# Out projection in halves, a group norm on token scalars, and two one-sided tiles

## The reference, cut to what matters

```python
xbc = silu(centred_dwconv(h @ w_in[:, o0:o1], ...))   # x 1024, B 256, C 256 channels
...
for o, gate in enumerate(gates):                      # hyena branch, twice
    z = gate * (fft_conv(z, kf[:, o]) + z * hy_bias[o])
y_hy = rmsnorm(z.reshape(b, L, 8, 128), hy_norm_w)    # 8 groups of 128 channels
y_ssd, s_f, s_b = ssd_branch(...)                     # state-space branch
out = concatenate([y_hy, y_ssd], -1) @ w_out          # 2048 x 2048
x = x + g1 * out
```

## Time and profile before

| what | value |
|---|---|
| median of 3 runs | 4664.4 us (4656.6 to 4666.23) |
| span of the profiled execution | 4666.4 us |
| its own time | not listed apart; the listed runs reach 4666.23 us |
| mean granted PE clock | 0.966 |
| busy share | PE 94%, PEld 79%, POOL 71%, DVE 57%, ACT 37% |
| inverse transforms end, out1 begins | 809.8 us, 846.1 us |
| last out1 matmul starts | 938.8 us |

### The profile page before, as it was taken

How to read it: one execution, slowest core, us unless ns; L and a number is a source line. 1 busy time by engine, 2 the same in 40 slices (tenths; PEclk the granted TensorE clock), 3 DMA queues, 4 the chain that set the end, 5 groups by cost and what they waited for, 6 DMA issues and landing times.

```text
span 4666.4 us, 65475 instructions
## 1 busy us (share of the span) xinstructions
PE 4367.9 (94%) x24574; PEld 3666.7 (79%) x24574; DVE 2647.6 (57%) x3815; ACT 1718.0 (37%) x1864; POOL 3296.1 (71%) x1312
## 2 busy tenths in 40 slices
PE   8898989789999999999989998999999899899997
PEld 1676755668888878888877886899888788788876
DVE  3326675365554575544254412598867857875784
ACT  1234432333333343434434332443333333333333
POOL 0347750668888877877867783887887787787776
PEclk9998979899999999999999998999999999999999
DMA  8346750445555544444544452444554454454443
GB/s 314 128 175 245 298 210 1 154 153 186 183 180 180 186 154 165 173 167 181 190 145 163 171 186 87 170 167 166 178 185 169 158 190 170 162 181 173 171 165 124
DMA packets 111126, 805.19 MB, mean 173 GB/s; under 512 B 12903, under 2 KB 13192, under 8 KB 14088
## 3 DMA queue, kind: packets, MB, share of 16 engines
q1 hardware_dynamic: 108720, 787.30, 46.8%
q10 hardware_dynamic: 2200, 14.90, 0.9%
HBM read 800.06 MB, written 2.10 MB: 172 GB/s over the span
## 4 chain that ended last, share of the span: by engine, by line
PE 34%; POOL 28%; issue 20%; DVE 7%; POOLq 0%; ACT 0%; DMA 0%; DVEq 0%; ACTq 0%
POOL w_lo L430 28%; PE psum L498 18%; PE psum L500 9%; DVE out_hl L2747 2%; PE psum L620 2%; DVE out_hl L2745 1%; DVE hid L2743 1%; PE psum L1145 1%; PE psum L487 1%; PE psum L488 1%; PE psum L489 1%; DVE mix_m L2002 0%; POOLq L427 0%; DVE chosen L2683 0%; DVE pick L2679 0%
## 5 line engine op out<-in xcount | busy, mean ns | idle before, releaser
L430 POOL TENSOR_TENSOR w_lo<-ring,w_hi 128x1024 fp32r<-128x1024 f32 x1216 | 2945.6, 2426 | 1219.5 <-ACT w_hi L1221 1218.5
L1221 ACT ACTIVATE w_hi<-ring 128x1024 fp32r<-128x1024 f32 x1240 | 1310.9, 1060 | 2175.4 <-PE psum L500 1920.9
L498 PE MATMUL psum<-hc_hl,w_hi 128*128 128x512 f32 x5184 | 1865.9, 404 | 82.8 <-DVE hc_hl L2177 24.5
L500 PE MATMUL psum<-hc_hl,w_lo 128*128 128x256 f32 x5184 | 1460.8, 282 | 0.0
L498 PEld LDWEIGHTS psum<-hc_hl,w_hi 128*128 128x128 f32 x5184 | 983.3, 190 | 325.2 <-issue 56.7
L500 PEld LDWEIGHTS psum<-hc_hl,w_lo 128*128 128x128 f32 x5184 | 989.0, 191 | 4.7 <-issue 4.5
L498 PE MATMUL psum<-out_hl,w_hi 128*128 128x512 f32 x2048 | 726.0, 399 | 30.7 <-DVE x L2757 27.3
L500 PE MATMUL psum<-out_hl,w_lo 128*128 128x256 f32 x2048 | 578.9, 283 | 0.0
L498 PEld LDWEIGHTS psum<-out_hl,w_hi 128*128 128x128 f32 x2048 | 388.5, 190 | 123.3 <-DVE x L2757 28.3
L500 PEld LDWEIGHTS psum<-out_hl,w_lo 128*128 128x128 f32 x2048 | 392.1, 191 | 0.0
L498 PE MATMUL psum<-hid_hl,w_hi 128*128 128x512 f32 x1024 | 363.9, 400 | 17.4 <-DVE hid_hl L2231 12.2
(11 more groups left out here) (439 smaller groups left out, 5509.9 us busy)
## 6 DMA issues: line engine op xcount, KB each, us to landing
ring<-stream SPq DMA_DIRECT2D x652, 1024.0 KB, 4.8
ring<-mixed SPq DMA_DIRECT2D x96, 1024.0 KB, 6.5
x<-x ACTq DMA_DIRECT2D x2, 2048.0 KB, 11.2
ctx_raw<-ctx ACTq DMA_DIRECT2D x1, 2048.0 KB, 9.6
mem_raw<-mem ACTq DMA_DIRECT2D x1, 2048.0 KB, 9.2
out<-x SPq DMA_DIRECT2D x4, 512.0 KB, 2.6
filt_w<-filt_w ACTq DMA_DIRECT2D x1, 1024.0 KB, 10.8
dft<-dft ACTq DMA_DIRECT2D x1, 1024.0 KB, 12.7
```

What stands on the lines that cost most here:

```text
L430: pool.tensor_tensor(w_lo[:, slot], ring[:, s, k], w_hi[:, slot].bitcast(F32), ALU.subtract).then_inc(lo_ready, 1)
L498: pe.matmul(psum[:, b, :].rearrange("p (s t) -> p s t", s=2), w_hi[:, slot, c], x_hl, start=start(c), stop=False, skip_group_check=True)
L500: m = pe.matmul(psum[:, b, 0:T], w_lo[:, slot, c], x_hl[:, 0], start=False, stop=stop(c), skip_group_check=True)
L1221: act.activation(w_hi[:, 2 * (s % 2) + h], ring[:, s, k], ACT.Copy).then_inc(hi_ready, 1)
```

## The change

- Out projection: tiles 0 to 3 are done in eight halves, first the state-space halves (blocks 8 to 15) of all four tiles, then their hyena halves. Each tile's PSUM bank stays open between. From tile 4 on the old loop runs. SP reloads a slot after its second half. DVE's first four additions wait for the later halves.
- Group norm of the hyena half: in two channel halves q, each with its own semaphores. PE multiplies the squares (as weights) with a column of ones, 8 products of one column, so that the sums lie by token on partitions, 8 numbers each. Mean, root and reciprocal work on [128, 8]. PE spreads the reciprocals to all partitions: 8 products of 128 columns with the identity. The scaled result is written in PSUM; ACT makes `h_hi` from it, DVE `h_lo`.
- xbc: tiles 10 and 11 (C) are computed for x alone: three 256-column matmuls per block, convolution and silu on 256 columns.
- Semaphores renamed and shared (group norm of both branches, value turning of the memory attention); no work differs there.

```diff
@@ sync
         for s in range(RING):
             slot_free(MIXED - RING + s)
             load(FIRST["out1"] + s, s)
-        with sp.Fori(FIRST["out1"] // RING + 1, N_TILES // RING) as i:
+        for s in range(RING):
+            sp.wait_ge(lo_ready, 2 * XBC + RING + s + 1)
+            load(FIRST["out1"] + RING + s, s)
+        with sp.Fori(FIRST["out1"] // RING + 2, N_TILES // RING) as i:
@@ gpsimd
+        for n in range(2 * RING):
+            t, h = n % RING, 1 - n // RING
+            pool.wait_ge(hi_ready, 2 * XBC + n + 1)
+            if n == 0:
+                pool.wait_ge(y_y, 4)
+            pool.tensor_tensor(w_lo[:, n % 4], ring[:, t, 8 * h:8 * h + 8], w_hi[:, n % 4].bitcast(F32),
+                               ALU.subtract).then_inc(lo_ready, 1)
@@ tensor, xbc
+                    if t >= XBC - 2:
+                        o = psum[:, t % RING, 0:T]
+                        pe.matmul(o, w_hi[:, slot, c], h_hi[:, k], start=k == 0, stop=False)
+                        pe.matmul(o, w_hi[:, slot, c], h_lo[:, k], start=False, stop=False)
+                        m = pe.matmul(o, w_lo[:, slot, c], h_hi[:, k], start=False, stop=k == KC - 1)
+                        continue
@@ tensor, after inverse(3)
+        def group_columns(q):
+            pe.wait_ge(gn_sq, q + 2)
+            for k in range(4):
+                for b in range(2):
+                    m = pe.matmul(psum[:, 4 + 2 * q, 2 * k + b:2 * k + b + 1], hy_sq[:, 4 * q + k, b * P:b * P + P],
+                                  const[:, ONES, 0:1], start=True, stop=True)
+            m.then_inc(gn_sum, 1)
+        def group_spread(q):
+            pe.wait_ge(gn_inv, q + 1)
...
+                    m = pe.matmul(psum[:, 4 + 2 * q + k // 2, c0:c0 + P], hy_n[:, q, n:n + 1].broadcast_to([P, P]),
+                                  sq(IDENT), start=True, stop=True)
+            m.then_inc(gn_spread, 1)
+        def out1_half(n):
+            t, h = n % RING, 1 - n // RING
+            pe.wait_ge(lo_ready, 2 * XBC + n + 1)
+            for c in range(8):
+                if n == RING and c % 4 == 0:
+                    pe.wait_ge(gn_out, c // 4 + 2)
...
-        group_norm_pe(0)
-        pe.wait_ge(gn_out, 1)
-        linear("out1", h_hl)
+        group_columns(0)
+        pe.wait_ge(gn_out, 1)
+        pe.wait_ge(y_zc, 8)
+        out1_half(0)
+        group_columns(1)
+        group_spread(0)
+        out1_half(1)
+        group_spread(1)
+        for n in range(2, 2 * RING):
+            out1_half(n)
+        linear("out1", h_hl, RING, KC - RING)
@@ scalar, after z_out_(3, 1)
+        def out1_split(n):
+            t, h = n % RING, 1 - n // RING
+            act.wait_ge(landed[t], FIRST["out1"] // RING * 16 + 16)
+            act.wait_ge(half_done, 2 * FIRST["out1"] + n - 3)
+            act.activation(w_hi[:, n % 4], ring[:, t, 8 * h:8 * h + 8], ACT.Copy).then_inc(hi_ready, 1)
...
-        group_norm_act(0, u[:, 0:8])
+        act.wait_ge(y_y, 2)
+        for n in range(RING):
+            out1_split(n)
+        half_square(0)        # waits y_new 3, squares u[:, 0:4]
+        half_square(1)        # waits y_new 4
         act.dma_start(x[:], a["x"]).then_inc(norm_in, 16)
-        split_stage("out1", ahead=2)
+        half_root(0)
+        half_root(1)
+        out1_split(4)
+        half_high(0)
+        out1_split(5)
+        half_high(1)
+        out1_split(6)
+        out1_split(7)
+        split_stage("out1", RING, KC - RING)
@@ vector, after next_z(3)
-        group_norm_dve(0)
...
+        half_mean(0)
+        half_inverse(0)
+        half_mean(1)
+        half_inverse(1)
+        half_scaled(0)        # 4 x [128, 256]: PSUM <- u, hy_norm, PSUM
+        half_scaled(1)
+        half_low(0)           # [128, 1024]: h_lo <- PSUM, h_hi
+        half_low(1)
@@ vector, residual (all out-projection additions)
-            with dve.Fori(0, n // RING - 1) as i:
+            for j in range(RING):
+                add(0, j, RING - 1 - j)
+            with dve.Fori(1, n // RING - 1) as i:
```

More of the change, by code:

```diff
@@ L327, in build @@
         "inverse", "new_z"))
-    gn_in, gn_sq, gn_sum, gn_ms, gn_rt, gn_out = (sem("gn_" + n) for n in ("in", "sq", "sum", "ms", "rt", "out"))
+    gn_sq, gn_sum, gn_ms, gn_rt, gn_out = (sem("group_norm_" + n) for n in ("sq", "sum", "ms", "rt", "out"))
+    gn_scaled, gn_hi, gn_inv, gn_spread = (sem("group_norm_" + n) for n in ("scaled", "hi", "inverse", "spread"))
     hid_ready = sem("hidden_ready")
@@ L840, in _ @@
         inverse(3)
[L842 to L847, removed]
-            m.then_inc(gn_sum, 1)
-        group_norm_pe(0)
-        pe.wait_ge(gn_out, 1)
-        linear("out1", h_hl)
+        def group_columns(q):
[4 more added lines that the diff above has]
+                                  const[:, ONES, 0:1], start=True, stop=True)
+            m.then_inc(gn_sum, 1)
+        def group_spread(q):
+            pe.wait_ge(gn_inv, q + 1)
+            for k in range(4):
+                for b in range(2):
+                    n = 2 * k + b
+                    c0 = (k % 2) * T + b * P
+                    m = pe.matmul(psum[:, 4 + 2 * q + k // 2, c0:c0 + P], hy_n[:, q, n:n + 1].broadcast_to([P, P]),
[7 more added lines that the diff above has]
+                    pe.wait_ge(gn_out, c // 4 + 2)
+                pe.matmul(psum[:, t, :].rearrange("p (s t) -> p s t", s=2), w_hi[:, n % 4, c], h_hl[:, :, 8 * h + c],
+                          start=h == 1 and c == 0, stop=False, skip_group_check=True)
+                m = pe.matmul(psum[:, t, 0:T], w_lo[:, n % 4, c], h_hi[:, 8 * h + c], start=False,
+                              stop=h == 0 and c == 7, skip_group_check=True)
+            m.then_inc(half_done, 1)
+        group_columns(0)
+        pe.wait_ge(gn_out, 1)
+        pe.wait_ge(y_zc, 8)
[7 more added lines that the diff above has]
+        linear("out1", h_hl, RING, KC - RING)
         norm_pe("x2")
@@ L942, in _ @@
             if n == 29:
-                group_norm_pe(1)
+                pe.wait_ge(gn_sq, 4)
+                for k in range(8):
+                    m = pe.matmul(psum[:, 4 + k // 2, (k % 2) * T:(k % 2) * T + T], sq(ONES), gn_q[:, k],
+                                  start=True, stop=True)
+                m.then_inc(gn_sum, 1)
         def dil_rotate(h, p):
@@ L1309, in xbc_silu @@
             act.wait_ge(bank_free, 4 + bank_of["xbc"] + t + 1)
-            act.activation(xbc[:, t], xbc[:, t], ACT.Silu).then_inc(s_silu, 1)
+            v = xbc[:, t, 0] if t >= XBC - 2 else xbc[:, t]
+            act.activation(v, v, ACT.Silu).then_inc(s_silu, 1)
         for t in range(2, XBC):
@@ L1539, in _ @@
             if n == 5:
-                act.wait_ge(gn_out, 2)
+                act.wait_ge(gn_out, 4)
                 act.dma_start(dil_mask[:], a["dil_mask"]).then_inc(s_tab, 16)
@@ L1912, in _ @@
         for t in range(XBC):
-            conv_base[0] = st.n - 4 * t
-            conv_tile(t // RING, t % RING, FIRST["xbc"], xbc[:, t].rearrange("p s t -> p (s t)"), "ssd_w", "ssd_b", XBC, True)
-            st.n += 4
+            pair = t < XBC - 2
+            conv_base[0] = st.n - (4 if pair else 2) * t
+            conv_tile(t // RING, t % RING, FIRST["xbc"],
+                      xbc[:, t].rearrange("p s t -> p (s t)") if pair else xbc[:, t, 0], "ssd_w", "ssd_b", XBC, pair)
+            st.n += 4 if pair else 2
             if t == 3:
@@ L2141, in _ @@
         st.settle()
-        dve.tensor_tensor(h_lo[:, 8:16], y_ssd[:], h_hi[:, 8:16].bitcast(F32), ALU.subtract).then_inc(g_out, 1)
-        dve.wait_ge(g_out, 1)
+        dve.tensor_tensor(h_lo[:, 8:16], y_ssd[:], h_hi[:, 8:16].bitcast(F32), ALU.subtract).then_inc(gn_out, 1)
+        dve.wait_ge(gn_out, 1)
         filter_parts(1)
@@ L2159, in _, with half_mean, half_inverse, half_scaled @@
         next_z(3)
[L2161 to L2170, removed]
-        group_norm_dve(0)
[L2172 to L2177, removed]
+        def half_mean(q):
+            dve.wait_ge(gn_sum, q + 2)
+            dve.tensor_scalar(hy_n[:, q], psum[:, 4 + 2 * q, 0:8], 1.0 / P, EPS, ALU.mult, ALU.add).then_inc(gn_ms, 1)
+        def half_inverse(q):
+            dve.wait_ge(gn_rt, q + 2)
+            dve.reciprocal(hy_n[:, q], hy_n[:, q]).then_inc(gn_inv, 1)
+        def half_scaled(q):
+            ps = flat[:, 2048 + 1024 * q:3072 + 1024 * q]
+            dve.wait_ge(gn_spread, q + 1)
+            for k in range(4):
+                m = dve.scalar_tensor_tensor(ps[:, T * k:T * k + T], u[:, 4 * q + k], col("hy_norm", 4 * q + k),
+                                             ps[:, T * k:T * k + T], ALU.mult, ALU.mult)
+            m.then_inc(gn_scaled, 1)
+        def half_low(q):
+            dve.wait_ge(gn_hi, q + 1)
+            dve.tensor_tensor(h_lo[:, 4 * q:4 * q + 4].rearrange("p k t -> p (k t)"),
+                              flat[:, 2048 + 1024 * q:3072 + 1024 * q],
+                              h_hi[:, 4 * q:4 * q + 4].bitcast(F32).rearrange("p k t -> p (k t)"),
```

(5 more changed lines are left out.)

63 lines of the change are left out of this document (33 added, 30 removed).

## The result

| what | before | with the change |
|---|---|---|
| median | 4664.4 us (4656.6 to 4670.82, 5 runs) | 4624.8 us (4618.79 to 4643.73, 5 runs) |
| ratio | | 0.9912 [0.9895, 0.9929] |
| profiled execution | span 4666.4 | span 4625.2, its own time 4627.06 |
| inverse transforms end | 809.9 us | 799.5 us |
| last out1 matmul starts | 938.84 us | 897.83 us |

Faster by 39.6 us by the medians and 41.2 by the two spans; forecast was 43.3. Of the 41.2, 41.0 are there when out1 ends (938.84 - 897.83). The interval of the ratio is 33 to 49 us, so the total alone can't tell 43.3 from 39.6.

The account below looks back on a forecast made before the run. PE, 94% busy, was taken as the bound, so gains come from less PE work or filled pauses. xbc 12.9 (10.2 + 1.3 + 1.4) plus tail 30.4 made 43.3 us: span 4623.1, median 4621, range 4610 to 4636.

Parts of the forecast that it names:

- The total and the sign: Whole program: faster by 43.3 us, median 4621; forecast itself had chance 0.73, faster by more than 9 us 0.95.
- xbc's matmuls, 10.2 us: xbc tiles 10 and 11: three narrow matmuls replace 0.68 us a block, 2 x 16 x 0.32 = 10.2 us saved.
- The 1.4 us of clock: Behind xbc's last convolution: pause falls from 2.97 to 1.7 us, so 1.4 us of half clock returns (bounds 0 and 1.4).
- They should follow: Mixed stage after xbc: it should follow the earlier start, passing on the sum of 12.9 us (bounds 11.5 and 12.9).
- the xbc gain is lost in the mixed stage: First rival, mixed stage: its loads or POOL sums set the end whatever PE does; 4634 us, chance 0.08.
- The lock: Tail: `u` (two SBUF inputs on DVE) waits for the POOL instruction under way; second u 1.6 us late, PE stalls 1.5.
- so I expect full clock: xbc's shortened pause: after a pause of 2.22 us PE ran its next 256-column matmul in 0.28 us, the full-clock value.
- the lock or the clock costs more: Second rival, tail: POOL's four halves hold DVE, or clock falls at the stall; up to 9.4 us more, 4630, chance 0.14.
- The tail, 30.4 us: Inverse transforms to out1's end: 908.6 against 938.96, 30.4 us saved, 2.5 of it late clock; bounds 21 and 31.9.
- Table load: ACT before the root: load of 1.28 us with nothing behind it; with the page's drain the sum is 41.9, not 43.3.
- What was costed at nothing: Tail: h copies covered with 1.2 us to spare before hyena half 4; reloads of 4.8 us covered by the eight halves.
- The slower rival: Out1: PE's clock does not hold, a half takes 2.3 us more, 73 us over 32 halves; 4694, chance 0.02.

Follow-up runs that it names:

- h1: The changed kernel with out1's second half put on PE ahead of the second group-norm column sums, POOL's lock left in place; 4625.29 us, one run.
- t1: The changed kernel without the narrow C tiles, so only the new tail (halves and group norm) against the kernel before; 4633.63 us, ratio 0.9927.
- p1: The changed kernel with two more POOL waits, so no POOL instruction lies over DVE's product writing the second `u`; 4626.2 us, ratio 0.9899.
- x1: The kernel before with only xbc's tiles 10 and 11 computed for x alone, tail as before; 4655.01 us, ratio 0.9977.
- x2: x1 with the old 512-column convolution of tiles 10 and 11, silu still 256 columns wide; 4657.1 us, one run.
- r1: The changed kernel run again without an edit; 4631.8 us, ratio 0.9919.
- r2: The changed kernel run again without an edit, beside z1 on the same chip, five rounds; 4624.03 us, ratio 0.9906.
- z1: The same kernel as k1 run again with five rounds, beside r2 on the same chip; 4621.01 us, ratio 0.9901.
- n1: The changed kernel with the new group norm, but out1 waits for all of h before any half; 4638.33 us, ratio 0.9942.
- q1: The changed kernel with out1's new order of halves, but the old group norm over [128, 2048]; 4643.62 us, ratio 0.9947.
- k1: p1 with ten more unused PE products in the pauses before the third and fifth native projection; 4624.32 us, ratio 0.9910.

## Why the prediction was right, and where not

- **The total and the sign are right**: 4621 forecast, 4624.8 measured, 43.3 us against 39.6. No rival took place as a whole; part of the first and part of the second did. Read by stages at the same pace of out1, the change gives 8.5 to 9.9 and 29.0, some 38 us, so both terms are a little too large; that the total came closer is in part luck.
- **xbc's matmuls, 10.2 us: right.** 0.12 us a matmul as in the earlier trace rows. From tile 9's convolution to the first projection it is 24.69 before and 13.14 after: 11.55 for the 11.5 of matmuls and last convolution.
- **The 1.4 us of clock: right in its place, undersized there, and in good part lost again.** The first two projections gained 1.7 to 2.9 us (15.77 and 17.0 to 14.08); over the first five the means differ by 1.4.
- **"They should follow", for the mixed stage, is the step that failed**, where of 12.9 us 8.5 arrive at the stage's end (9.9 with h1). The rival "the xbc gain is lost in the mixed stage" had the right place and a third of its price. Shown: the wait for the third load stays as long as it was, and the projection behind it now runs at half clock in most traces; products in the pauses before the third and fifth projection shorten the head by 3.6 us. Not shown: that this is the part that was lost, for the kernel before was not run with these products and has its own half-clock stretches at the fifth projection; and where the rest goes. The trace of h1, 6.6 us quicker in the head with unchanged code there, points at a second cause that the prediction left out for this stage: DVE held by POOL's sums, the lock of the earlier trace rows. The traces of this stage scatter by about as much as was lost.
- **The lock is as predicted, its price has other parts.** The earlier trace rows foretold that `u` would be held by POOL's instruction: the first 1.85 (1.9 forecast), the second 2.51 for 1.23, 1.22 again when POOL stays away. Forecast were a 2.8 us `u` and a stall of 1.5; measured were 2.51 and 0.83. The step "so I expect full clock" (taken for xbc from the earlier trace rows, where 2.22 us did no harm) was carried over silently to this stall: behind it 1.7 us were lost at half clock in three of four traces. The pause of 0.83 us has one-column products right behind it and, but for one half of out1, ahead of it; the pause of 2.22 us stood between 512- and 256-column ones. Why the clock fell after the shorter one, and not in t1, no run here tells. Together 2.7 for 1.5; the rival "the lock or the clock costs more" had this mechanism, and up to 9.4 us for it.
- **The tail, 30.4 us: 30.6 in the profile, 29.0 in the two repeats.** The difference of the last two is out1's pace (last section). With before's pace, and the half clock, the like-for-like gain is 29.0; t1, with before's pace and full clock, gives 30.6. So the layout was right to 0.3 us with a stall of 0.83 for 1.5, and the 1.7 of clock is what it lacked.
- **Table load: the row was right.** 804.80 to 806.08, the root at 806.09. The drain of some 1.38 us that the Trainium skill (ScalarE: Activation LUTs, "What ACT_TABLE_LOAD costs") has beside the load isn't there, in this place either, and the 1.4 us that the page would have cost didn't come.
- **What was costed at nothing stayed hidden**: both `h_lo` are done at 818.9, and half 4 starts at 820.2, 1.3 us to spare where 1.2 were forecast; a reload takes 4.8 to 4.9 us as in the earlier trace rows, and PE waits for no landing in out1.
- **The slower rival did not come near**: the granted clock is 1.00 in each stretch of the changed kernel's trace that was read between 812 and 894 us.

## What to carry to other kernels

When a serial chain of small steps stands between two long PE stages, look for a half of the next stage whose inputs are already there, and shorten the chain until it fits behind that half: norm and order gave 18.8 and 12.0 us, and neither alone the 30.6. Cost each pause on PE twice, once for its length and once for products behind it at half clock, which came in three of four traces here; filling the pause with useful work (h1) was as good as removing its cause (p1). A gain ahead of a stage with waits of its own (here loads, and DVE held by POOL) arrived only in part, and a half-clock stretch that it removes can come back one pause later. A stage that scatters by several us from trace to trace needs several traces of both kernels before such a loss is given a cause.

## What the hardware showed unexpectedly

**PE has two paces at full granted clock.** In out1 PE is the bound, so ACT's splits show its time for one half. The change and its first repeat, ACT in the same place:

```profile
856.55 1.06 ACT L1276 ACTIVATE w_hi<-ring 128x1024 fp32r<-128x1024 f32 x1 [1.71 <-PE psum L512]
859.32 1.06 ACT L1276 ACTIVATE w_hi<-ring 128x1024 fp32r<-128x1024 f32 x1 [1.71 <-PE psum L512]
862.10 1.06 ACT L1276 ACTIVATE w_hi<-ring 128x1024 fp32r<-128x1024 f32 x1 [1.71 <-PE psum L512]
```

```profile
854.35 1.06 ACT L1276 ACTIVATE w_hi<-ring 128x1024 fp32r<-128x1024 f32 x1 [1.76 <-PE psum L512]
857.18 1.06 ACT L1276 ACTIVATE w_hi<-ring 128x1024 fp32r<-128x1024 f32 x1 [1.77 <-PE psum L512]
860.01 1.06 ACT L1276 ACTIVATE w_hi<-ring 128x1024 fp32r<-128x1024 f32 x1 [1.77 <-PE psum L512]
```

A half takes 2.775 or 2.825 us. Of the fourteen traces eight have 2.825 in out1 (both of the kernel before, x1, x2, r1, r2, t1, z1) and six 2.775 (the change, p1, n1, q1, k1, h1); nothing lies between, and after the stage's first few halves it doesn't change. Over the 30 halves behind the second spread it is 1.6 us, all of the difference between tails of 98.4 and 100.0. In a later stage (1300 to 1340 us) the same program again shows either value: 2.827 in one trace of the kernel before, 2.774 in the other. What chooses it no run here tells. From out1's end to the end of the program, where all kernels are the same, the times go from 3719.8 us (r1) to 3737.4 (p1), which is more than most terms of the sum; how much of that is this pace wasn't measured. Terms of a few microseconds were therefore read from one stage of the traces and not from the total.
